# Third gate tile ahead of the fourth value block, a reordered layer boundary, and a last residual pair on GpSimd

## What is computed

```python
def hybrid_layer(x, positions, ...):
    h = rms_norm(x, g_mix_pre)
    proj = h @ w_in              # latents, attention inputs, 3 x 1024 gate logits
    o_a = mla_branch(...) @ w_o_mla      # 8 heads, causal, low-rank q and kv
    o_b = swa_branch(...) @ w_o_swa      # window of 128, sinks
    o_c = stick_breaking_branch(...) @ w_o_sb
    gates = sigmoid(gate_logits + b_gate).reshape(B, S, 3, D)
    mixed = gates[:, :, 0] * o_a + gates[:, :, 1] * o_b + gates[:, :, 2] * o_c
    x = x + rms_norm(mixed @ w_out, g_mix_post)
    h = rms_norm(x, g_mlp_pre)
    u = square(relu(h @ w_up))
    return x + rms_norm(u @ w_down, g_mlp_post)
```

## Time and profile before

| | us |
|---|---|
| median of three timed runs (lowest, highest) | 1727.54 (1726.42, 1728.59) |
| the profiled execution's own time | 1728.18 |
| its span, first to last instruction | 1726.3 |
| TensorE (PE) busy | 1700.1 (98%) |
| VectorE (DVE) busy | 1107.3 (64%) |
| ScalarE (ACT) busy | 855.0 (50%) |
| GpSimd (POOL) busy | 150.5 (9%) |
| SyncE's queue of weights | 147.42 MB, 24.7% of 16 DMA engines' time |

### The profile page before, as it was taken

One profiled execution on the slowest core, in us unless ns is written; L12 is line 12 of the kernel. 1 busy time (PEld: TensorE's weight loads), 2 busy tenths in 40 slices (PEclk: granted clock), 3 DMA queues, 4 the chain that ended last, 5 costly groups with the idle time before them and its releaser, 6 DMA issues.

```text
span 1726.3 us, 21789 instructions
## 1 busy us (share of the span) xinstructions
PE 1700.1 (98%) x8581; PEld 1435.6 (83%) x8581; DVE 1107.3 (64%) x1498; ACT 855.0 (50%) x1203; POOL 150.5 (9%) x142
## 2 busy tenths in 40 slices
PE   8999999999999999999999999999999999999997
PEld 6888888888898888888888888888888988888886
DVE  8887887775566534364597777977754665344545
ACT  7576566665355414131466755766644554232223
POOL 0111211111100000000001111111111000000000
PEclk9999999999999999999999999999999999999999
DMA  4121122222432222222321211122224122222222
GB/s 151 66 72 60 60 74 71 75 75 75 140 116 74 98 98 98 98 98 98 117 85 65 77 62 62 62 74 74 74 86 165 68 98 98 98 98 98 98 98 74
DMA packets 47495, 152.09 MB, mean 88 GB/s; under 512 B 5153, under 2 KB 9633, under 8 KB 47394
## 3 DMA queue, kind: packets, MB, share of 16 engines
q1 hardware_dynamic: 45664, 147.42, 24.7%
q10 hardware_dynamic: 1730, 3.28, 0.5%
HBM read 146.49 MB, written 4.19 MB: 87 GB/s over the span
## 4 chain that ended last, share of the span: by engine, by line
PE 83%; issue 7%; DVE 6%; ACT 3%; POOL 1%; DMA 0%; DVEq 0%; SPq 0%; POOLq 0%; ACTq 0%
PE bank L596 77%; PE bank L601 3%; PE bank L853 1%; PE bank L904 1%; POOL mix L2328 1%; ACT w_hi L1056 1%; DVE w_lo L1600 1%; PE bank L700 0%; DMA x<-in_x 0%; DVE fb L1849 0%; DVE hf L1647 0%; ACT dn L1113 0%; ACT dn L1111 0%; DVE h_lo L1635 0%; DVE of L1722 0%
## 5 line engine op out<-in xcount | busy, mean ns | idle before, releaser
L596 PE MATMUL bank<-h_hi,w_hi 128*128 128x512 f32 (+1 forms) x1224 | 476.5, 389 | 6.9 <-DVE h_lo L1635 2.9
L596 PE MATMUL bank<-h_lo,w_hi 128*128 128x512 f32 (+1 forms) x1224 | 471.8, 385 | 0.0
L596 PE MATMUL bank<-h_hi,w_lo 128*128 128x512 f32 (+1 forms) x1224 | 471.7, 385 | 0.0
L1056 ACT ACTIVATE w_hi<-raw 128x1024 fp32r<-128x1024 f32 (+2 forms) x269 | 271.0, 1012 | 220.2 <-DMA raw<-in_w 219.7
L1600 DVE TENSOR_TENSOR w_lo<-raw,w_hi 128x1024 fp32r<-128x1024 f32 (+2 forms) x269 | 316.6, 1180 | 61.6 <-ACT w_hi L1056 55.0
L596 PEld LDWEIGHTS bank<-h_hi,w_hi 128*128 128x128 f32 x1224 | 230.1, 188 | 57.0 <-issue 7.0
L596 PEld LDWEIGHTS bank<-h_hi,w_lo 128*128 128x128 f32 x1224 | 230.0, 188 | 46.6
L596 PEld LDWEIGHTS bank<-h_lo,w_hi 128*128 128x128 f32 x1224 | 230.1, 188 | 44.6 <-issue 1.2
L596 PE MATMUL bank<-u_hi,w_hi 128*128 128x512 f32 (+1 forms) x560 | 208.1, 372 | 0.0
L596 PE MATMUL bank<-u_hi,w_lo 128*128 128x512 f32 (+1 forms) x560 | 207.7, 371 | 0.0
L596 PE MATMUL bank<-u_lo,w_hi 128*128 128x512 f32 (+1 forms) x560 | 207.7, 371 | 0.0
(11 more groups left out here) (265 smaller groups left out, 2752.9 us busy)
## 6 DMA issues: line engine op xcount, KB each, us to landing
raw<-in_w SPq DMA_DIRECT2D x251, 512.0 KB, 3.2
x<-in_x SPq DMA_DIRECT2D x16, 256.0 KB, 3.3
side_raw<-in_w SPq DMA_DIRECT2D x6, 512.0 KB, 4.9
x_spill<-x ACTq DMA_DIRECT2D x8, 256.0 KB, 2.5
x<-x_spill SPq DMA_DIRECT2D x8, 256.0 KB, 3.2
out_y<-x SPq DMA_DIRECT2D x8, 256.0 KB, 2.1
raw<-in_w SPq DMA_DIRECT2D x8, 192.0 KB, 2.4
raw<-in_w SPq DMA_DIRECT2D x8, 128.0 KB, 2.3
```

Of the source, the lines that this page charges most:

```text
L596: mm = pe.matmul(o, s, m, start=start and i == 0 and j == 0, stop=last and i == n - 1 and j == 2, skip_group_check=True)
L1056: act.activation(chunk_in(gc, w_hi, side_hi)[:, 0:w], chunk_in(gc, raw, side_raw)[:, 0:w], ACT.Copy)\
```

## The change

Three edits.

1. In all engines' orders, tile `gate 0,2` comes before value block 3. TensorE runs `mla_shift(0)` after its sixth block. ScalarE converts value blocks 0 to 2 ahead of query 1, and block 3 after `soft_hi(0)`. VectorE makes the low value blocks in order, scales `gate 0,2` before `split(11)`, and does value block 3 after `probs_lo(0)`.
2. At the boundary ScalarE's `down_part(5, 1)` comes after the first two `next_in`, and VectorE's `gather` of that block after the first `layer_lo`.
3. At the end GpSimd does the last pair of the second half (multiplication in place in y, then addition to x), and SyncE waits for it before the last store. VectorE does three pairs there.

```diff
@@ order
-        elif h == 1:
-            seq += values[-1:]
         if 0 < h < HEADS - 1:
             seq += own("gate", 0, h + 1)
+        if h == 1:
+            seq += values[-1:]
@@ sync
-                        sp.wait_ge(*res((2 + h) * KT // 2 + t // 2 + 1))
+                        if h and t == KT - 2:
+                            sp.wait_ge(last_pair, 2)
+                        else:
+                            sp.wait_ge(*res((2 + h) * KT // 2 + t // 2 + 1))
@@ tensor
-                        if halfway and t == KT // 2:
+                        if halfway and t == half:
...
+                    tile(("gate", 0, 2), h_hi, h_lo, None, lambda: mla_shift(0), half=KT - 2)
                     mla_v(NB - 1)
-                    tile(("gate", 0, 2), h_hi, h_lo, None, lambda: mla_shift(0))
@@ scalar
-                    mla_q(1)
-                    mla_v(NB - 1)
                     for j in range(NB - 1):
                         mla_v(j)
+                    mla_q(1)
                     soft_exp(0)
                     split(C["gate", 0, 2] + 2)
                     soft_hi(0, s_f[:, :], p_hi[:, :])
+                    mla_v(NB - 1)
...
-                    down_part(HALF, 1)
                     if now[0] + 1 == DEPTH:
+                        down_part(HALF, 1)
...
                             if t == 1:
+                                down_part(HALF, 1)
                                 down_part(HALF + 1, 1)
@@ vector
-                    cols, n1, pairs = HALVES[h], n0 + KT // 2 * h, KT // 2
+                    cols, n1, pairs = HALVES[h], n0 + KT // 2 * h, KT // 2 - (0 if then else h)
...
-                    dve.wait_ge(*mv_h((j + 1) % NB + 1))
+                    dve.wait_ge(*mv_h(j + 1))
...
-                        dve.wait_ge(*mv_l(1))
+                        dve.wait_ge(*mv_l(NB))
                         dve.sem_inc(free_of(("mla_v", j)), 1)
...
                     mla_q(1)
-                    mla_v(NB - 1)
+                    mla_v(0)
                     mla_qk(1)
-                    for j in range(NB - 1):
+                    for j in range(1, NB - 1):
                         mla_v(j)
+                    scaled(("gate", 0, 2), mix[:, 2, :])
                     split(C["gate", 0, 2] + 2)
                     probs_lo(0, s_f[:, :], p_hi[:, :], p_lo[:, :])
-                    scaled(("gate", 0, 2), mix[:, 2, :])
+                    mla_v(NB - 1)
...
+                    def first_lo_gather(t, h):
+                        layer_lo(t, h)
+                        if t == 0:
+                            gather(MPOST, HALF, 1)
+
                     for p in range(KT // 2 + 1):
-                        residual(p, 0, KT, layer_lo if more else None)
+                        residual(p, 0, KT, (first_lo_gather if p == 1 else layer_lo) if more else None)
                         if p == 0:
-                            down_part(HALF, 1)
+                            down_sum(HALF, 1)
+                            if not more:
+                                gather(MPOST, HALF, 1)
@@ gpsimd
+                pool.wait_ge(*rs_step(2 * SUM_OF[MPOST, 1] + 2))
+                late, both = y[:, KT - 2:KT, HALF_B], rstd[:, HALF_B].unsqueeze(1).broadcast_to([P, 2, SEQ // 2])
+                pool.tensor_tensor(late, late, both, ALU.mult).then_inc(last_pair, 1)
+                pool.wait_ge(last_pair, 1)
+                to = x[:, KT - 2:KT, HALF_B]
+                pool.tensor_tensor(to, to, late, ALU.add).then_inc(last_pair, 1)
```

More of the change, by code:

```diff
@@ L344, in signal @@
             return Signal(sem(name), per, now)
+        last_pair = sem("last_pair")
         whi = signal("w_hi_ready", CHUNKS)
@@ L635, in weight, with tile @@
                     return (chunk_in(gc, w_hi, side_hi)[:, rows], chunk_in(gc, w_lo, side_lo)[:, rows])
-                def tile(name, hi, lo, ready=None, halfway=None, cols=ALL):
+                def tile(name, hi, lo, ready=None, halfway=None, cols=ALL, half=KT // 2):
                     c = chunk_of(name)
@@ L1947, in down, with down_sum @@
                             dve.tensor_tensor(y[:, t, :], y[:, t, :], rsq[:, :], ALU.mult).then_inc(y_rsq.sem, 1)
-                def down_part(t, h):
+                def down_sum(t, h):
                     g = GROUPS - 1
@@ L1955, in down_part @@
                        .then_inc(free_of(name), 1)
+                def down_part(t, h):
+                    down_sum(t, h)
                     gather(MPOST, t, h)
```

## The result

The changed kernel takes 1737.91 us (median of six runs, 1736.85 to 1739.11), the kernel before, on the same chip, 1728.18 (six runs). The ratio is 1.0056 with a 95% interval of 1.0045 to 1.0067: 9.7 us slower. Run again beside other runs of the kernel before it gave 1738.55 against 1728.34, 1.0060 (1.0048 to 1.0073). The profiled execution took 1736.93 us, its span is 1735.1, 8.8 more than the span before.

A forecast was written before the change was run, and what follows sets the result against it. PE bounds the kernel, busy 1700.1 of 1726.3 us. Terms 6.4 + 1.8 - 0.6 + 1.3 = +8.9 gave 1737.1 for the profiled execution, 1736.5 for the median; range 1731.5 to 1740.5.

The forecast's parts named there:

- Edit 1, the gain: In each layer's heads, the gate tile starts at 55.31 instead of 57.56, winning 1.56 us per layer.
- Edit 1, the cost: Late refill of chunk 11 holds ScalarE, then the keys of query 2; net loss 3.2 us per layer, +6.4 in all.
- The second small wait: Behind the late keys, VectorE reads out query 2 later; the next gate tile is 3.2 us late, the keys 2.81.
- The clock: PE's 4.4 us gap ahead of the keys of query 2 lowers its clock: 0.9 us per layer, +1.8 in all.
- Rival (a): The clock holds in both layers' gaps: +7.1 us, 1734.7; chance 0.20.
- Edit 2: At the layer boundary, PE's wait falls from 1.30 to 0.74 us: -0.6 us.
- Edit 3: In the tail, GpSimd and VectorE passes collide over SBUF; last store 1.2 us later, term +1.3 us.
- Rival (c): The tail does not collide, the rest as forecast: +6.7 us, 1734.2; chance 0.12.
- (b): Chunk 11's refill does not hold ScalarE up in the heads: 1725.1, or 1722.9 without the tail collision; chance 0.13.
- (d): Edit 1 acts as forecast in one layer only: +3.2 to +4.8 us, 1730.8 to 1732.4; chance 0.05.

The follow-up runs named there:

- the runs whose clock stayed at 1.00: The changed kernel plus unread matmuls on TensorE ahead of the keys of query 2: 14 in both layers, 1738.11 us; 18, 1737.75; 18 in one layer, 1737.36 and 1737.49.
- edit 1 alone: The kernel before with only the gate-tile and value-block reordering: 1737.13 us against 1728.12, ratio 1.0055.
- 14 matmuls, second layer: Second layer of the changed kernel with 14 unread matmuls put ahead of the keys of query 2 in both layers: 1738.11 us, ratio 1.0059.
- edit 2 alone: The kernel before with only the boundary reordering on ScalarE and VectorE: 1727.97 us, one run.
- GpSimd's multiplication alone: The kernel before with GpSimd doing only the multiplication of the last pair and VectorE the addition: 1728.93 us, one run.
- the moved conversion: The changed kernel with chunk 11's conversion placed later on ScalarE and VectorE: 1727.40 us, ratio 0.9997; also without edit 3, 1725.85, ratio 0.9988.

## Why the prediction was right, point by point

**The forecast** was 1736.5 for the median, range 1731.5 to 1740.5, slower. The sign, the range and the mechanism hold; 1737.91 and 1738.55 lie 1.4 and 2.1 above it. The profiled execution, for which the sum was made, was forecast at 1737.1 and took 1736.93. That closeness is in part luck: this execution began 0.67 us earlier, which no term foresaw; without it 8.8 would have been 9.5, and the terms, 8.9, are 0.6 short of that. The miss of the median is the step from that execution to the median: I took 0.64 off, from three runs with a median of 1727.54, but six runs gave 1728.18 and the later sets 1728.12 to 1728.57, so the execution of before lay on its median, and that of the changed kernel a us below its own.

**Edit 1, the gain.** Right in both layers: the tile starts where the value block did. The refill went out 6.95 us behind the tile's start (54.64 to 61.59), forecast 7.01 (55.31 to 62.32).

**Edit 1, the cost.** Each link was there: issue, landing in 3.26, conversion, low parts, bank. The keys come 2.62 and 2.54 later than before; I had 2.81, and PE's idle time is 4.1 instead of 4.4. The second small wait was put at 0.4 (3.2 less 2.81) and was too small; the runs whose clock stayed at 1.00 show it: the tile comes 3.19 after the keys there, before 2.60, so it is 0.59, which makes up for keys that are less late than forecast. Without the clock the term is 3.2 per layer, as forecast. The lateness then died out, as expected: from the scores of head 0 in one layer to those in the next it takes 857.11 us against 853.44, which is the first layer's 4.29 less the boundary's 0.57. That the conversion ahead of the probabilities is the link that counts was argued from the order of the calls; moving it showed it, by 10 us.

**The clock.** Forecast 0.9 per layer net of the small wait. Measured as the difference between 4.27 and 4.18 in the changed kernel and 3.19: 1.08 and 0.99, up to 1.64 in the run with edit 1 alone. The fall came with each of the eight gaps of 4.0 to 4.5 us ahead of these keys. Rival (a), that the clock holds, did not happen. The size was in part luck: 0.9 was chosen between 0 and 2.1, and the fall came later than in the tail, at 1.00 still from 68 to 69 us, so that the low stretch lay wholly behind the gap. The 15 matmuls from the keys to the tile then took 4.27 us instead of 2.88 (3.19 less a wait of 0.31 ahead of the tile), 1.39 more, and the wait of 0.31 fell away. The Trainium skill, "TensorE: Matmul & The Clock Gate", section "What's actually happening", has the clock throttled by default and lifted by activity, and says that the moment varies from run to run; the traces agree, the low stretch behind the first layer's gap being some 3 us long in the changed kernel and 5 with edit 1 alone, where the clock had fallen inside the gap.

**Edit 2.** Forecast a wait of 0.74 instead of 1.30; it is 0.73, and it lasted.

**Edit 3.** The mechanism was right, the term a little low: +1.3 forecast, +1.53 in the trace, 1.55 to 1.8 between runs. The passes were played through to +1.2 for the last store, which is exact (1.21); the last transfer added 0.3 where I had taken 0.1. The Trainium skill, "SBUF — State Buffer", section "Who interferes with whom", has a VectorE instruction with two SBUF inputs contend with a GpSimd instruction that reads SBUF, and calls what they share an exclusive lock; the trace agrees, 1.07 us more for VectorE for each of GpSimd's two passes. Rival (c) is out.

**Rivals (b) and (d).** (b) would decide at ScalarE's start on chunk 11, at 62.8 or earlier. It came at 64.87, which is 65.54 with the 0.67 us by which this execution began earlier. (d): the layers' losses differ by 0.17 us (4.29 and 4.12).

## What to carry to other kernels

Before a tile is moved, ask which transfers are tied to its end: a refill that waits for the last user of a buffer moves with it, and every conversion that stands in a fixed place of an in-order engine turns a late transfer into a stall of what is queued behind it. If such a conversion isn't urgent, put it behind what is. And work handed to an idle engine is a gain only if the two do not need the same access to memory; where each pass of one holds up a pass of the other, as in this tail (2.36 us instead of 1.29), the helper makes both slower.

## What the runs showed that I had not expected

- **The clock fell in shorter gaps too.** It fell to 0.50 behind a gap of 2.21 us in mid-kernel (14 matmuls, second layer), and behind PE's wait for low parts of the input near 11 us in the runs of edit 2 alone (gap 2.23), GpSimd's multiplication alone (2.24), and the moved conversion (2.55, and 2.07 without edit 3). In the other profiles that gap was 0.61 to 2.02 us and the granted clock stayed at 1.00. This and the gap itself shift all that follows: the scores of head 0 start anywhere from 50.61 to 52.35. In the two profiles of the changed kernel they start at 50.91 and 52.02, which is 1.11 of the 1.7 us between their spans, and a reason to compare distances.
- **A packet of instructions in a landing.** Chunk 11 took 4.5 and 4.7 us instead of 3.1 to 3.8 in the two profiles in which a packet of 16 KB of instructions lay in the middle of its transfer; at 3.2 to 3.5 it was not late in the three in which the packet came near the transfer's end. The Trainium skill, "Runtime: NRT & Kernel Launch", section "Instruction fetch mechanics", has each sequencer fetch its instructions in blocks of 16 KiB over a DMA queue of its own, at a cost that is mostly hidden. The two late landings, 1.3 and 1.5 us over the 3.2 of the changed kernel, may be a case where it isn't hidden; no run here shows that they come from the packet.
- **A landing isn't a constant.** Apart from those two, the landing of the same 512 KB took 3.2 to 3.8 us in the first layer and 3.1 to 3.3 in the second. Why the layers differ stays open.
